# Decoder step on one Trainium2 core: value stores moved to the end of the attention stage, two value pages put behind four key pages, key quarters and three vector instructions put in another order

## The chip, the cores and the metric

The kernel runs on one core of one Trainium2 chip. The metric is the device time of one execution in microseconds (us), as the median over the runs of one version; lower is better. Five engines work side by side in a core: TensorE (PE; the loading of its weights is listed as PEld), VectorE (DVE), ScalarE (ACT), GpSimd (POOL) and SyncE (SP). Each takes its own instructions in the order in which they are written and waits on semaphores for the others. Transfers between the main memory and the on-chip memories are issued by SP and by ACT, each on a queue of its own (q1 and q10 in the profile), and are carried out by 16 DMA engines that both queues share.

## What is computed

One inference step of a small decoder, for one prompt of 512 tokens with 16 learned tokens ahead of it, and for 8 running sequences of 8 new tokens each with 1024 cached tokens. Layer one is a retention layer, layer two an attention layer with forget gates; each is followed by an MLP with a squared ReLU. Cut to what matters here:

```
x = x + retention_out(retention(...)); x = x + mlp(x)          # layer 1
k, v, logf = fox_shared_kv(x)          # new keys and values, both also outputs
q, gate = fox_in(x)
# prompt: causal attention of 16 heads over k, v
# 8 sequences: attention over 1024 cached rows, cache_k[page_table] and
#   cache_v[page_table] (8 pages of 128 rows each), and over the new k, v
p = softmax(q k^T * scale + cum_q - cum_k, masked);  o = p v
x = x + (o * sigmoid(gate)) @ w_fox_out
x = x + mlp(x)                         # layer 2
mlp(x) = square(relu(rms_norm(x, g) @ w_up)) @ w_down
```

All 592 tokens (64 new ones of the sequences, 16 learned, 512 of the prompt) go through the weights together. The outputs are the new activations, the retention states, and the new keys, values and log forget values.

## The kernel before, in words

The program is written out by hand, engine by engine: `block.sync` (SP), `block.gpsimd`, `block.tensor`, `block.scalar` (ACT) and `block.vector` (DVE) each hold the list of what their engine does, and the waits between them. Nothing reorders it later. Products of 32-bit numbers are made of three TensorE products of a high and a low part of each operand (`unit`, `unit_tok`, `unit_by_sums`): ACT rounds the high part of a weight block (`w_hi`), POOL or DVE subtracts it for the low part (`split`, `weight_low`).

**The attention stage** comes after the last block of the weights for the values (block N_V + 3). It is a pipeline of 9 rounds, b from 0 to 8, of 4 slots each, i from 0 to 3. A slot takes one of 32 pieces of the prompt's attention (j, a pair of heads and a block of 128 queries, by `pair_at`) and two of the 8 key pages of sequence b, and beside that the value pages of sequence b - 1.

- A *key page* holds 128 cached rows of 1024 numbers. `k_page` (L668) fetches it in four quarters of 128 KB, each a transfer of its own: quarter `a` takes four of the heads, in pieces of 1 KB, to partitions 32a to 32a + 31. There are 4 buffers for key pages. DVE waits for all four quarters and turns the page (`turn_page`, L2321), which raises `k_turned`; SP waits for that in `k_next` (L679) before it issues the page that is four further on. PE takes two turned pages at a time in `pair_scores`.
- A *value page* of 512 KB is one transfer (`v_page`, L674). There are 8 buffers. SP issues the first eight; the later ones ACT issues in `v_next`, when PE has used a buffer.
- In SP's list the first four key pages come first, then (when the last block of weights is done) the eight first value pages, the seventh behind a wait for `qb_done` and the eighth behind one for `kn_done`, and then key page 4 and the others through `k_next`.
- ACT issues the outputs before its own loop: the new log forget values and keys (`out_f`, `out_k`), and, when the last values have left PSUM, the new values (`out_v`, L1743): 2048, 64 and 256 KB. It then makes the exponentials (`exp`, L1750) and scales the probabilities with the inverse row sums (`normed_probs`, L1758).
- DVE, in each slot (from L2360): the row maxima of piece j (`maximum`), a page, the reciprocals of the row sums (`inverse_sums`, L2308), another page, and the gating of the piece before. In round 0 the first two slots hold no piece; slot 2 holds piece 0 and pages 4 and 5.
- Behind its loop ACT rounds the first block of the output projection (`w_hi(Blk(N_OUT))`), and waits for all stores of `out_f` and `out_v`.

**The MLP** is done in four chunks. In the last three the first matrix is multiplied by a scheme with seven block products in place of eight (`unit_by_sums` on PE; on DVE the list in `chunk`, from L2143). A chunk has four such units, j from 0 to 3. DVE adds a product in three steps, of which PE waits for the second and third (`prod_read`), and between them it makes the weights of the next unit: their sums, the low parts (`weight_low`, L2064, where j < 3) and the low parts of the sums (`sums_low`, L2070). There are two MLPs, so the unit j = 0 comes six times.

## Time and profile before

| | |
|---|---|
| time, median of 3 runs | 2080.22 us (2076.53 to 2080.82) |
| the profiled execution's own time | 2071.38 us |
| its span, first to last instruction | 2069.6 us |
| mean granted TensorE clock | 0.977 |
| PE busy | 1949.4 us, 94% of the span |
| DVE, ACT, POOL busy | 1049.0, 706.6 and 475.8 us |
| read from and written to the main memory | 210.77 and 26.12 MB |
| time of the packets of SP's queue and of ACT's queue, as a share of 16 engines | 29.5% and 8.1% |

The profile is that of one execution. A row of a timeline gives the start and the duration in us, the engine, the line of the program, the operation and its tiles; in brackets stands how long the engine was idle just before and what ended the idle time. "SPq" and "ACTq" are the engines' own sequencers, where transfers are issued; an issue row says how long issuing took, not when the data landed. Spans of matmuls overlap, so start times say more than sums of durations.

### The profile page before, as it was taken

To read this page: it belongs to the slowest core of one execution; us is meant where nothing else is said; L and a number is where in the kernel's file an instruction comes from. 1 tells how busy PE (TensorE), PEld (TensorE's weight loads), DVE (VectorE), ACT (ScalarE), POOL (GpSimd) and SP (SyncE) were. 2 spreads that over 40 slices of the span, in tenths; PEclk is the share of its full clock that TensorE was granted. 3 is DMA by queue.
4 is the path that set the end of the run, shared out by engine and by line. 5 is a ranking of instruction groups with operands and counts; after the bars stand their busy time and mean duration, and the time that the engine had idled before them with its cause. 6 is when DMAs were issued, how large, how long until landed. Compare 5 with 4: busy or idle time off the path is not lost.

```text
span 2069.6 us, 35725 instructions
## 1 busy us (share of the span) xinstructions
PE 1949.4 (94%) x14855; PEld 1789.2 (86%) x14855; DVE 1049.0 (51%) x1170; ACT 706.6 (34%) x898; POOL 475.8 (23%) x106
## 2 busy tenths in 40 slices
PE   3999999999998999999999999789998999999998
PEld 3988988988878999999999999645555999999998
DVE  2456245245346666464542535465664566736452
ACT  3132222222224425152432432144444332425241
POOL 1221521511505321212132232000000332021211
PEclk9999999999999999999999999879999999999999
DMA  4233233243342222222322221679997322322231
GB/s 137 82 111 135 92 126 129 83 135 120 102 153 82 82 80 84 82 87 76 109 78 82 63 65 60 228 192 268 280 266 204 95 81 80 102 82 81 81 102 46
DMA packets 197349, 239.13 MB, mean 116 GB/s; under 512 B 16419, under 2 KB 168355, under 8 KB 197027
## 3 DMA queue, kind: packets, MB, share of 16 engines
q1 hardware_dynamic: 171138, 183.25, 29.5%
q10 hardware_dynamic: 26000, 53.48, 8.1%
q8 instruction: 98, 1.61, 0.3%
q0 software_dynamic: 80, 0.52, 0.1%
q14 instruction: 33, 0.26, 0.0%
HBM read 210.77 MB, written 26.12 MB: 114 GB/s over the span
## 4 chain that ended last, share of the span: by engine, by line
PE 58%; issue 26%; DVE 5%; POOL 4%; DMA 4%; SPq 2%; ACT 1%; ACTq 0%; POOLq 0%; DVEq 0%
PE PS L782 10%; PE PS L784 10%; PE PS L783 10%; POOL w_lo L728 4%; PE PS L798 4%; PE PS L800 4%; PE PS L799 4%; DMA k_page<-in_cache_k 3%; PE PS L861 3%; PE PS L863 2%; PE PS L862 2%; PE PS L1303 1%; PE PS L1258 1%; SPq L671 1%; PE PS L1204 1%
## 5 line engine op out<-in xcount | busy, mean ns | idle before, releaser
L728 POOL TENSOR_TENSOR w_lo<-w_raw,w_hi 128x2048 fp32r<-128x2048 f32 (+1 forms) x101 | 474.6, 4699 | 1561.2 <-ACT w_hi L1407 1561.2
L1407 ACT ACTIVATE w_hi<-w_raw 128x2048 fp32r<-128x2048 f32 (+1 forms) x101 | 191.8, 1899 | 630.1 <-PE PS L784 418.8
L782 PE MATMUL PS<-hidden_hi,w_hi 128*128 128x296 f32 (+1 forms) x1024 | 304.4, 297 | 0.7 <-DVE hidden_tmp L2092 0.6
L784 PE MATMUL PS<-hidden_hi,w_lo 128*128 128x296 f32 (+1 forms) x1024 | 304.7, 298 | 0.0
L783 PE MATMUL PS<-hidden_lo,w_hi 128*128 128x296 f32 (+1 forms) x1024 | 304.2, 297 | 0.0
L782 PE MATMUL PS<-x_hi,w_hi 128*128 128x296 f32 (+1 forms) x896 | 271.0, 302 | 9.2 <-DVE x_lo L1856 6.1
L783 PE MATMUL PS<-x_lo,w_hi 128*128 128x296 f32 (+1 forms) x896 | 269.4, 301 | 0.0
L784 PE MATMUL PS<-x_hi,w_lo 128*128 128x296 f32 (+1 forms) x896 | 268.6, 300 | 0.0
L861 PE MATMUL PS<-w_hi,x_hi 128*128 128x256 f32 x800 | 226.5, 283 | 0.4 <-DVE fox_gate L2242 0.4
L863 PE MATMUL PS<-w_lo,x_hi 128*128 128x256 f32 x800 | 225.6, 282 | 0.0
L862 PE MATMUL PS<-w_hi,x_lo 128*128 128x256 f32 x800 | 225.3, 282 | 0.0
L782 PEld LDWEIGHTS PS<-hidden_hi,w_hi 128*128 128x128 f32 x1024 | 193.1, 189 | 1.6 <-issue 1.0
L783 PEld LDWEIGHTS PS<-hidden_lo,w_hi 128*128 128x128 f32 x1024 | 193.2, 189 | 0.0
L784 PEld LDWEIGHTS PS<-hidden_hi,w_lo 128*128 128x128 f32 x1024 | 192.6, 188 | 0.0
L782 PEld LDWEIGHTS PS<-x_hi,w_hi 128*128 128x128 f32 x896 | 170.3, 190 | 11.8 <-DVE x_lo L1856 7.4
L783 PEld LDWEIGHTS PS<-x_lo,w_hi 128*128 128x128 f32 x896 | 170.2, 190 | 0.3
L784 PEld LDWEIGHTS PS<-x_hi,w_lo 128*128 128x128 f32 x896 | 170.1, 190 | 0.0
L861 PEld LDWEIGHTS PS<-w_hi,x_hi 128*128 128x128 f32 x800 | 151.3, 189 | 1.1 <-issue 1.0
L863 PEld LDWEIGHTS PS<-w_lo,x_hi 128*128 128x128 f32 x800 | 151.4, 189 | 0.0
L862 PEld LDWEIGHTS PS<-w_hi,x_lo 128*128 128x128 f32 x800 | 151.2, 189 | 0.0
L2092 DVE TENSOR_TENSOR hidden_tmp<-PS,inv_root 128x1184 f32<-128x1184 f32 (+1 forms) x32 | 44.0, 1374 | 178.3 <-PE PS L784 178.0
L1414 ACT ACTIVATE w_hi<-w_raw 128x2048 fp32r<-128x2048 f32 x24 | 46.0, 1918 | 202.9 <-DVE w_raw L2055 202.9
(288 smaller groups left out, 3893.9 us busy)
## 6 DMA issues: line engine op xcount, KB each, us to landing
w_raw<-in_w_mlp_up SPq DMA_DIRECT2D x32, 1024.0 KB, 5.4
w_raw<-in_w_mlp_down SPq DMA_DIRECT2D x32, 1024.0 KB, 5.1
k_page<-in_cache_k SPq DMA_DIRECT2D x256, 128.0 KB, 6.6
v_page<-in_cache_v ACTq DMA_DIRECT2D x56, 512.0 KB, 8.5
w_raw<-in_w_ret_in SPq DMA_DIRECT2D x24, 1024.0 KB, 5.3
sample_state<-in_state_ret SPq DMA_DIRECT2D x32, 512.0 KB, 4.9
out_state_ret_sample<-sample_state ACTq DMA_DIRECT2D x32, 512.0 KB, 4.4
w_raw<-in_w_ret_out SPq DMA_DIRECT2D x16, 512.0 KB, 3.4
```

What stands on the lines that cost most here:

```text
L728: pool.tensor_tensor(lo, raw, hi.bitcast(F32), ALU.subtract).then_inc(lo_done, 1)
L782: pe.matmul(o, wh[:, w], xh[:, t, cols], start=(t == 0), stop=False)
L783: pe.matmul(o, wh[:, w], xl[:, t, cols], start=False, stop=False)
L784: last = pe.matmul(o, wl[:, w], xh[:, t, cols], start=False, stop=(t == kt - 1))
L798: pe.matmul(o, wh[:, t], xh[:, t], start=first and t == 0, stop=False, skip_group_check=True)
L799: pe.matmul(o, wh[:, t], xl[:, t], start=False, stop=False, skip_group_check=True)
L800: last = pe.matmul(o, wl[:, t], xh[:, t], start=False, stop=(t == 3), skip_group_check=True)
L861: pe.matmul(o, XH[:, t, tok], wh[:, c], start=start, stop=False, skip_group_check=skip)
L862: pe.matmul(o, XL[:, t, tok], wh[:, c], start=False, stop=False, skip_group_check=skip)
L863: return pe.matmul(o, XH[:, t, tok], wl[:, c], start=False, stop=(t == KT - 1), skip_group_check=skip)
L1407: act.activation(part(WH[n.slot], n), part(WR[n.slot], n), ACT.Copy).then_inc(hi_done, 1)
L1414: act.activation(WH[n.slot][:], WR[n.slot][:], ACT.Copy).then_inc(hi_done, 1)
```

## The change

Five edits, none of which changes what is computed.

1. `out_v` is issued by ACT behind its attention loop, ahead of `w_hi(Blk(N_OUT))`, on a semaphore of its own (`v_stored`). DVE waits for it ahead of the second MLP, whose buffers lie where the values were.
2. SP issues six value pages, then key pages 4 to 7 (as their buffers come free), then value pages 6 and 7, then the rest.
3. The quarters of a key page are issued in the order 0, 2, 1, 3.
4. In round 0 DVE makes the reciprocals of a piece ahead of the first of the slot's two pages.
5. In the MLP's unit j = 0 DVE makes the low parts of the next weights behind the second addition of the product, not ahead of it.

```
+        v_stored = sem("v_stored")
...
-            def k_page(kn, quarters=range(4)):
+            def k_page(kn, quarters=(0, 2, 1, 3)):
...
-                    k_page(NPAGE * b + p + NKS, range(4))
+                    k_page(NPAGE * b + p + NKS)
...
-            for i in range(NVS):
-                if i == 6:
-                    sp.wait_ge(qb_done, 1)
-                if i == 7:
-                    sp.wait_ge(kn_done, 1)
+            for i in range(6):
                 v_page(i)
             for b in range(DB + 1):
                 for p in range(4):
                     k_next(b, p)
+                if b == 0:
+                    sp.wait_ge(qb_done, 1)
+                    v_page(6)
+                    sp.wait_ge(kn_done, 1)
+                    v_page(7)
...
-            for dst, src in out_v:
-                act.dma_start(dst, src).then_inc(out_stored, 16)
...
+            for dst, src in out_v:
+                act.dma_start(dst, src).then_inc(v_stored, 16)
             w_hi(Blk(N_OUT))
-            act.wait_ge(out_stored, 16 * 6)
+            act.wait_ge(out_stored, 16 * 3)
...
-            act.wait_ge(out_stored, 16 * 6)
+            act.wait_ge(v_stored, 16 * 3)
...
-                        if j < 3:
+                        if 0 < j < 3:
                             weight_low(m + 1)
                         dve.wait_ge(sum_done, 2 * u + 1)
                         dve.wait_ge(prod_ready, 6 * u + 3)
                         dve.tensor_tensor(tmp[:, 1, 1], c, tmp[:, 0, 1], ALU.add).then_inc(prod_read, 1)
+                        if j == 0:
+                            weight_low(m + 1)
...
+                    if live(j) and b == 0:
+                        inverse_sums(j)
                     if k:
                         turn_page(NPAGE * b + 2 * i)
-                    if live(j):
+                    if live(j) and b > 0:
                         inverse_sums(j)
...
             roots(3)
+            dve.wait_ge(v_stored, 16 * 3)
             mlp(N_MLP1, 1)
```

SP's list at the start of the attention stage, before (key pages 4 and 5 go into the buffers k_page_144 and k_page_145; v_page_148 to v_page_155 are the eight buffers of value pages):

```order
L676 DMA v_page_152<-in_cache_v 128x1024
...
L676 DMA v_page_153<-in_cache_v 128x1024
...
L676 DMA v_page_154<-in_cache_v 128x1024
...
L676 DMA v_page_155<-in_cache_v 128x1024
...
L671 DMA k_page_144<-in_cache_k 32x4x256
```

and in the changed kernel:

```order
L677 DMA v_page_153<-in_cache_v 128x1024
...
L672 DMA k_page_144<-in_cache_k 32x4x256
...
L672 DMA k_page_145<-in_cache_k 32x4x256
...
L672 DMA k_page_146<-in_cache_k 32x4x256
...
L672 DMA k_page_147<-in_cache_k 32x4x256
...
L677 DMA v_page_154<-in_cache_v 128x1024
...
L677 DMA v_page_155<-in_cache_v 128x1024
```

Four key pages, 16 quarters, now stand ahead of the last two value pages.

DVE's list in round 0, slots 2 and 3, before:

```order
L2304 TENSOR_REDUCE neg_max<-PS 128x1
L2321 STREAM_TRANSPOSE k_page_t<-k_page_144 128x1024
L2308 RECIPROCAL row_inv<-row_sum 128x2
L2321 STREAM_TRANSPOSE k_page_t<-k_page_145 128x1024
L2302 TENSOR_TENSOR PS<-PS,c_fox_sb 128x128
```

and in the changed kernel:

```order
L2308 TENSOR_REDUCE neg_max<-PS 128x1
L2312 RECIPROCAL row_inv<-row_sum 128x2
L2325 STREAM_TRANSPOSE k_page_t<-k_page_144 128x1024
L2325 STREAM_TRANSPOSE k_page_t<-k_page_145 128x1024
L2306 TENSOR_TENSOR PS<-PS,c_fox_sb 128x128
```

The reciprocal no longer stands behind a page that has yet to arrive.

DVE's list in the MLP's unit j = 0 (hidden_tmp is the product, w_lo the next unit's weights), before:

```order
L2156 TENSOR_TENSOR hidden_tmp_89<-PS,hidden_tmp_89 128x296
L2064 TENSOR_TENSOR w_lo_55<-w_raw_51,w_hi_54 128x2048
...
L2161 TENSOR_TENSOR hidden_tmp_89<-PS,hidden_tmp_89 128x296
...
L2164 TENSOR_TENSOR hidden_tmp_89<-PS,hidden_tmp_89 128x296
...
L2070 TENSOR_TENSOR w_sum_lo_108<-w_sum_109,w_sum_hi_107 128x1536
```

and in the changed kernel:

```order
L2158 TENSOR_TENSOR hidden_tmp_89<-PS,hidden_tmp_89 128x296
...
L2163 TENSOR_TENSOR hidden_tmp_89<-PS,hidden_tmp_89 128x296
L2066 TENSOR_TENSOR w_lo_55<-w_raw_51,w_hi_54 128x2048
...
L2168 TENSOR_TENSOR hidden_tmp_89<-PS,hidden_tmp_89 128x296
...
L2072 TENSOR_TENSOR w_sum_lo_108<-w_sum_109,w_sum_hi_107 128x1536
```

The long subtraction stands between the second and the third addition now, not between the first and the second.

## Rows read from the trace of the kernel before

**Rows 1.** The waits of PE, whole span: engine, tile, line, releaser: us, times, longest.

```profile
PE PS L1221 <- ACT probs L1758: 16.0, 7, 14.9
...
PE PS L798 <- DVE hidden_tmp L2161: 7.6, 6, 1.3
```

**Rows 2.** Timeline of DVE at the start of the attention stage.

```profile
1349.33 1.25 DVE L2321 STREAM_TRANSPOSE k_page_t<-k_page 128x1024 f32<-128x1024 f32 x1 [17.02 <-DMA k_page<-in_cache_k]
...
1351.59 1.25 DVE L2321 STREAM_TRANSPOSE k_page_t<-k_page 128x1024 f32<-128x1024 f32 x1 [0.97 <-DMA k_page<-in_cache_k]
```

**Rows 3.** Timeline of ACT at the same place, ACTq its issues.

```profile
1327.54 1.17 ACTq L1744 DMA_DIRECT2D out_v_prompt<-fox_v  x2
1328.74 1.52 ACTq L1744 DMA_DIRECT2D out_v_sample<-fox_v  x1
...
1333.78 0.20 ACT L1750 ACTIVATION_READ_ACCUMULATOR probs<-PS,neg_max 128x1 f32 x1
1350.66 0.72 ACT L1758 ACTIVATE probs<-probs,row_inv 128x144 f32<-128x144 f32 x2 [16.68 <-DVE row_inv L2308]
```

**Rows 4.** Timeline of SP's issues at the same place.

```profile
1325.02 11.85 SPq L676 DMA_DIRECT2D v_page<-in_cache_v  x8
1338.48 14.52 SPq L671 DMA_DIRECT2D k_page<-in_cache_k  x19
```

**Rows 5.** The transfers from 1326 to 1344: all packets.

```profile
DMA packets 2188, 6.72 MB, mean 373 GB/s; under 512 B 469, under 2 KB 595, under 8 KB 2188
```

**Rows 6.** Timeline of PE behind the wait: pages 4 and 5, next piece's scores.

```profile
1352.89 1.93 PE L1258 MATMUL PS<-k_page_t,q_blocks 128*32 128x256 f32 x16 [0.77 <-DVE k_page_t L2321]
...
1356.10 1.01 PE L1200 MATMUL PS<-cum_parts,negsel_r 128*128 128x384 f32 x2
```

**Rows 7.** Timeline of DVE: maxima of a sequence's scores, rounds 2, 3, 4 and 8.

```profile
1395.15 1.29 DVE L2328 TENSOR_REDUCE neg_max<-PS 128x1 f32<-128x1088 f32 x1
1424.92 1.29 DVE L2328 TENSOR_REDUCE neg_max<-PS 128x1 f32<-128x1088 f32 x1
1459.13 1.29 DVE L2328 TENSOR_REDUCE neg_max<-PS 128x1 f32<-128x1088 f32 x1
...
1580.51 1.29 DVE L2328 TENSOR_REDUCE neg_max<-PS 128x1 f32<-128x1088 f32 x1
```

**Rows 8.** Transfers from 1346 to 1350, key quarters alone: all packets.

```profile
DMA packets 992, 0.90 MB, mean 226 GB/s; under 512 B 110, under 2 KB 992, under 8 KB 992
```

**Rows 9.** Transfers from 1603 to 1608, weight blocks alone: all packets.

```profile
DMA packets 1790, 1.82 MB, mean 363 GB/s; under 512 B 16, under 2 KB 1790, under 8 KB 1790
```

**Rows 10.** Timeline of DVE in one MLP unit j = 0.

```profile
781.54 0.47 DVE L2156 TENSOR_TENSOR hidden_tmp<-PS,hidden_tmp 128x296 f32<-128x296 f32 x1 [0.94 <-ACT hidden_tmp L1608]
781.92 2.28 DVE L2064 TENSOR_TENSOR w_lo<-w_raw,w_hi 128x2048 fp32r<-128x2048 f32 x1
784.12 0.46 DVE L2161 TENSOR_TENSOR hidden_tmp<-PS,hidden_tmp 128x296 f32<-128x296 f32 x1
784.70 0.47 DVE L2164 TENSOR_TENSOR hidden_tmp<-PS,hidden_tmp 128x296 f32<-128x296 f32 x1
```

**Rows 11.** Timeline of PE in the same unit.

```profile
783.06 0.30 PE L800 MATMUL PS<-x_hi,w_lo 128*128 128x296 f32 x1
784.63 0.41 PE L798 MATMUL PS<-x_hi,w_hi 128*128 128x296 f32 x1 [1.27 <-DVE hidden_tmp L2161]
...
786.37 0.30 PE L798 MATMUL PS<-x_hi,w_sum_hi 128*128 128x296 f32 x1
```

**Rows 12.** Timelines of ACT, POOL and PE at the end of the attention stage.

```profile
1594.39 1.89 ACT L1407 ACTIVATE w_hi<-w_raw 128x2048 fp32r<-128x2048 f32 x1
...
1596.36 4.54 POOL L728 TENSOR_TENSOR w_lo<-w_raw,w_hi 128x2048 fp32r<-128x2048 f32 x1 [298.65 <-ACT w_hi L1407]
...
1605.57 0.58 PE L782 MATMUL PS<-fox_y_hi,w_hi 128*128 128x288 f32 x1 [2.24 <-DVE fox_y_lo L2389]
```

**Rows 13.** Windows, 1352 to 1373: engines' busy us, granted clock, DMA share, GB/s.

```profile
1352.00:1373.00 21.00, 20.18 (x119) 11.50 (x119) 12.37 (x24) 7.98 (x22) 0.00 (x0) 0.59 0.67 168
```

## The prediction

> **What bounds the kernel now.** I read four views, in this order. First the waits of PE, since PE is busy for 94% of the span and time can only be had where it is not: one wait of 14.9 us stands out, on ACT's scaled probabilities (L1758), and one kind comes six times, 7.6 us in all, on DVE's second addition in the MLP (L2161) [rows 1]. Second the timelines of the engines around the long wait, to follow it back. DVE had the row maxima of the first piece done at 1332.3 and then stood for 17.02 us in front of the transpose of key page 4, until its data were there at 1349.33 [rows 2]. The reciprocal that ACT needed stood behind that transpose: ACT had the exponentials done at 1333.98 and waited 16.68 us [rows 3]. SP shows why the page was late: its first quarter was issued at 1338.48 only, behind eight value pages whose issues took from 1325.02 on, while ACT issued the stores of the values from 1327.54 on [rows 4, 3]. All told 6.72 MB went through the DMA engines from 1326 to 1344, at 373 GB/s [rows 5].
>
> Third the pace of the rounds behind it. The maxima of a sequence's scores come once a round. The round from 1395.15 to 1424.92 took 29.77 us; the six rounds from 1395.15 to 1580.51 took 185.36 us, which is 6.7 us more than six of the short one [rows 7]. So this stretch is bound by the engines' own chain for most of the time, and by late key pages for 6.7 us at most. Fourth the timelines of one MLP unit j = 0, for the waits that come six times [rows 10, 11].
>
> **Stores and value pages at the start.** Behind the change six value pages stand ahead of key page 4, not eight, and the stores (2048 + 64 + 256 KB = 2.42 MB) are gone from there. Two value pages are 1.05 MB. 3.47 MB at the 373 GB/s of [rows 5] are 9.3 us, by which key page 4 comes earlier. The other key pages keep their distance to it, since quarters alone drain at 226 GB/s [rows 8], 2.3 us a page, about the 2.26 us between the transposes of pages 4 and 5 [rows 2]. What PE does next hangs on page 5: its product of pages 4 and 5 began at 1352.89, the next piece's scores at 1356.10 [rows 6]; all of that moves with page 5. I take **9.3 us**. The bounds: 2.8 us, if the stores ran in time that SP's issues left free and only the two value pages count; 14.9 us, the whole wait of PE.
>
> Value pages 6 and 7 land later now, but PE wants them in round 1, some 30 us on: nothing. Key page 8 is new behind them, 2.8 us of transfers. Before, it was asked for when page 4 was turned (1349.33 + 1.25 [rows 2]) and is turned in round 1, behind maxima of scores that PE only began at 1356.10 [rows 6]; 5.5 us and the length of the scores lie between, of which the page itself takes 2.3; what is left covers the 2.8 about. Nothing, with 1.5 us as the upper end.
>
> **Reciprocals first.** In round 0 ACT and PE now get piece 0 done while the pages are on their way. But the product of pages 4 and 5 stands next in PE's list [rows 6], so the path still waits for page 5: I give it nothing beyond the 9.3 us. It has a price: page 6 is turned behind the second reciprocal, so behind the second pair of exponentials; I put that at 1.25 us, the length of the transpose with which it changes place [rows 2]. The product of pages 6 and 7 comes only behind the scores that began 3.2 us after page 4 and 5's [rows 6], which hides it.
>
> **Order of the quarters.** Nothing in the trace shows another order, so this is bounded. Key quarters and weight blocks come in pieces of the same 1 KB; the quarters, on 32 partitions each, drain at 226 GB/s [rows 8], weight blocks on 128 at 363 GB/s [rows 9]. Whatever costs the quarters that factor of 1.6 may be eased when one quarter's neighbours in the queue lie elsewhere. The upper end in the rounds is the 6.7 us above, because then the chain of the engines binds; the lower end is nothing, or a loss (the third rival). Even a tenth off a page is 8 x 0.23 = 1.8 us a round, more than most rounds have over 29.77, so I take a value nearer to the upper end: **4 us**.
>
> The Trainium skill, page "SBUF — State Buffer", section "Door 1: The DMA port swizzle", says that partitions 0 to 63 reach no more ports than 0 to 31, and that 64 to 127 reach the other half. By that rule the old order sends two quarters in a row to one half of the ports, the new order alternates, and the whole upper end could come (second rival). The same page, section "Can I just issue two DMAs to hit both halves?", speaks against it: two transfers at once, one on each half, were only 6% faster than one. By that 6% a page would save 0.14 us, an estimate, and the sum below would be nearer to 2062. The rows show the gap between the two shapes, and nothing of the order.
>
> **The MLP unit.** PE needs the second addition when its product ends, at 783.06 + 0.14 = 783.20, and the third 1.74 us later (784.63 to 786.37 is such a product) [rows 11]. Before, the second addition stood behind 2.28 us of low parts and ended at 784.58; PE began at 784.63, and the next product at 786.37. Now the second addition can start 0.58 us after the first started (the distance of second and third, 784.12 to 784.70 [rows 10]), at 782.12, and ends at 782.58, ahead of PE. The low parts follow from 782.50 to 784.78, the third addition ends at about 785.17, and PE goes on at 785.22, having waited some 0.3 us. That is 1.15 us less than 786.37. DVE's list from there is as early as before, so nothing behind it is later. Six units [rows 1], **6.9 us**, in a stage where PE has nothing else to wait for. The bounds: nothing, and the 7.6 us of the row.
>
> **The stores at the end.** ACT now issues three stores ahead of rounding the first output block. Issuing took 1.17 + 1.52 us [rows 3]. POOL finished its part at 1600.90 and PE began that block at 1605.57, behind another wait [rows 12]: 4.67 us of room. The transfers, 6.5 us at the rate above, go beside the weights of blocks that PE reaches some 15 us later. DVE's new wait comes some 50 us later. Nothing, unless issuing takes over 4.7 us; then the excess is lost, 3 us at most by a like queue.
>
> **The sum.** 9.3 + 4 + 6.9 = 20.2 us. The profiled execution took 2071.38 us and would take 2051.2; it lay 8.8 us under the median of 2080.22, and I take the difference over to that: **2060.0 us**. What a measurement of this kernel can tell from no change is about 0.2%, 4.2 us.
>
> **Rivals.**
> 1. *The stores were not what delayed the page.* SP's value pages went out one by one over 11.85 us [rows 4]; if that pace is SP's own, only two issues fall away. For it: the issues are evenly spread. Against it: the DMA engines moved 373 GB/s all that time [rows 5], so that they were hardly waiting for SP. Then 2.8 + 4 + 6.9 = 13.7, 2066.5 us. 13%.
> 2. *The quarters run at the rate of weight blocks.* A page takes 1.44 us in place of 2.32: the 6.7 us go whole, and pages 4 and 5 come 1.8 us earlier still. 9.3 + 1.8 + 6.7 + 6.9 = 24.7, 2055.5 us. For it: the factor of 1.6 [rows 8, 9]. 
> 3. *Slower: the new order makes key quarters slower.* The place is the rounds 1 to 8, 56 key pages, where little room is left. If a page takes longer by d, some 56 x d are lost, and from d = 0.29 us (an eighth of 2.32) on the 16.2 us of the other edits are gone; at a quarter, 0.58 us, 32 are lost and 2096 us come out. For it: the four quarters of a page are neighbouring KB of the same rows, and the new order reads them in jumps. Against it: all four are issued within 3 us or so either way, and both orders read the same pieces. 4%.
> 4. *The MLP edit only moves the wait*, to the third addition, for instance because the subtraction runs longer beside the second's readers. Then 13.3, 2066.9 us. For it: by my sum 0.3 us of waiting stays there anyway. Against it: all durations are measured and none changes. 8%.
>
> The clock is open too: from 1352 to 1373 the granted clock was 0.59 [rows 13], mostly the lower of its levels of 1.2 and 2.4 GHz, behind the long idle of PE. A shorter idle may keep less of it low, at most some 5 us for the better; I count nothing, but let the range reach there.
>
> **How the numbers follow.** The forecast has 60%, the rivals 13, 12, 4 and 8, and 3 are left for no visible effect. The range of 2050 to 2070 holds the forecast with its ends (order of the quarters nothing: 2064; with a late key page or a late end: 2067), rivals 1, 2 and 4, and on the low side the second with part of the clock; some 1 in 7 is left out. Faster by over 0.2%: 0.92; within: 0.04; slower: 0.04.
>
> **What would show it.** Right: DVE's wait ahead of page 4 of about 7 to 8 us, not 17; ACT's scaling of the first piece within a us of its exponentials; no wait of PE on the second addition, and one of 0.3 us on the third; in the stretch of the rounds a mean round between 29.8 and 30.9 us; PE's first output block still released by DVE. Wrong: page 4 transposed later than 1344 on the old clock; a stretch of only key quarters below 226 GB/s; PE's first output block released by POOL.

## The result and the profile after

Four runs of the changed kernel gave a median of 2049.55 us (2047.84 to 2056.13), four of the kernel before 2080.52 us (2076.53 to 2087.0): a ratio of 0.9854, 95% interval 0.9821 to 0.9887. The forecast was 2060.0 us, 2050 to 2070: the direction is right, the gain larger, the time 0.45 us below the range. In a later set with more runs (11 and 28) the ratio was 0.9895 [0.9864, 0.9926], a gain of 21.8 us where 20.2 were forecast. The kernel before spreads by itself, from 2060 to 2094 us over 91 later runs, and the time goes with the mean granted TensorE clock of the run: 0.980 in the shortest, 0.965 in the longest, a correlation of -0.89 over the 91.

The profiled executions took 2071.38 and 2048.63 us, spans 2069.6 and 2046.8. The difference by places: DVE's first page turns, the start of the attention stage, came 6.2 us earlier (1326.65, now 1320.42); from there to the first maxima of a sequence's scores passed 28.08 us, not 37.77; the seven rounds between the first and the last such maxima took 214.84 us, not 216.09; and what follows 483.46, not 489.09. 6.2 + 9.7 + 1.3 + 5.6 = 22.8 us. Ahead of the attention stage and behind it only the MLP edit acts, and 6.2 + 5.6 = 11.8 us is more than its 6.9; what is over belongs to these two executions (the last sections).

DVE's timeline at the start of the attention stage, changed kernel:

```profile
1320.42 4.58 DVE L2325 STREAM_TRANSPOSE k_page_t<-k_page 128x1024 f32<-128x1024 f32 x4
...
1327.78 0.17 DVE L2312 RECIPROCAL row_inv<-row_sum 128x2 f32<-128x2 f32 x1 [1.70 <-ACT probs L1750]
1333.65 1.25 DVE L2325 STREAM_TRANSPOSE k_page_t<-k_page 128x1024 f32<-128x1024 f32 x1 [5.70 <-DMA k_page<-in_cache_k]
1335.67 1.25 DVE L2325 STREAM_TRANSPOSE k_page_t<-k_page 128x1024 f32<-128x1024 f32 x1 [0.78 <-DMA k_page<-in_cache_k]
```

These answer to [rows 2]: the wait ahead of page 4 is 5.70 us, not 17.02 (7.4 with the wait that now comes first, for the exponentials that the reciprocal needs). Page 5 is turned 15.25 us after the first pages; before it was 24.94. On ACT's timeline the scaling of the first piece stands 0.23 us behind the exponentials, where [rows 3] show 16.68:

```profile
1327.98 0.72 ACT L1758 ACTIVATE probs<-probs,row_inv 128x144 f32<-128x144 f32 x2 [0.23 <-DVE row_inv L2312]
```

What PE waits for now, whole span (columns as in [rows 1]):

```profile
PE PS L1260 <- DVE k_page_t L2325: 6.5, 1, 6.5
...
PE PS L1223 <- ACT probs L1758: 1.2, 6, 0.2
PE PS L800 <- DVE hidden_tmp L2168: 1.1, 4, 0.3
```

The 14.9 us on the probabilities are gone, and 6.5 us on pages 4 and 5 have come in their place. The waits on the second addition are gone, and the third has four, none over 0.3 us, as forecast. SP's issues at the same place, against [rows 4]:

```profile
1318.79 5.88 SPq L677 DMA_DIRECT2D v_page<-in_cache_v  x6
1325.45 9.68 SPq L672 DMA_DIRECT2D k_page<-in_cache_k  x16
1335.90 1.48 SPq L677 DMA_DIRECT2D v_page<-in_cache_v  x2
```

The rounds, by the maxima as in [rows 7], on DVE's timeline (first, third to seventh, and last):

```profile
1348.50 1.29 DVE L2332 TENSOR_REDUCE neg_max<-PS 128x1 f32<-128x1088 f32 x1
...
1411.73 1.29 DVE L2332 TENSOR_REDUCE neg_max<-PS 128x1 f32<-128x1088 f32 x1
1441.49 1.29 DVE L2332 TENSOR_REDUCE neg_max<-PS 128x1 f32<-128x1088 f32 x1
1471.24 1.29 DVE L2332 TENSOR_REDUCE neg_max<-PS 128x1 f32<-128x1088 f32 x1
1501.00 1.29 DVE L2332 TENSOR_REDUCE neg_max<-PS 128x1 f32<-128x1088 f32 x1
1530.76 1.29 DVE L2332 TENSOR_REDUCE neg_max<-PS 128x1 f32<-128x1088 f32 x1
1563.34 1.29 DVE L2332 TENSOR_REDUCE neg_max<-PS 128x1 f32<-128x1088 f32 x1
```

Four rounds in a row take 29.75 or 29.76 us, the length of the shortest round of before; the mean of seven is 30.7 (29.8 to 30.9 forecast).

The unit j = 0 of the MLP, DVE's timeline and then PE's, against [rows 10, 11]:

```profile
778.70 0.47 DVE L2158 TENSOR_TENSOR hidden_tmp<-PS,hidden_tmp 128x296 f32<-128x296 f32 x1 [0.94 <-ACT hidden_tmp L1610]
779.29 0.47 DVE L2163 TENSOR_TENSOR hidden_tmp<-PS,hidden_tmp 128x296 f32<-128x296 f32 x1
779.67 2.28 DVE L2066 TENSOR_TENSOR w_lo<-w_raw,w_hi 128x2048 fp32r<-128x2048 f32 x1
781.87 0.46 DVE L2168 TENSOR_TENSOR hidden_tmp<-PS,hidden_tmp 128x296 f32<-128x296 f32 x1
```

```profile
782.38 0.41 PE L800 MATMUL PS<-x_hi,w_sum_hi 128*128 128x296 f32 x1 [0.24 <-DVE hidden_tmp L2168]
```

The second addition starts 0.59 us after the first (0.58 forecast); PE waits 0.24 us for the third. And the end of the stage, ACT's issues and then PE, against [rows 12]:

```profile
1576.76 0.41 ACTq L1810 DMA_DIRECT2D out_v_prompt<-fox_v  x1
...
1577.20 0.52 ACTq L1810 DMA_DIRECT2D out_v_prompt<-fox_v  x1
1577.76 1.05 ACTq L1810 DMA_DIRECT2D out_v_sample<-fox_v  x1
```

```profile
1588.07 0.58 PE L784 MATMUL PS<-fox_y_hi,w_hi 128*128 128x288 f32 x1 [2.24 <-DVE fox_y_lo L2395]
```

The first output block is still released by DVE, behind the same 2.24 us. The stores cost nothing there.

### The profile page after: what moved, and what is told of

Its sections match the earlier page's. It is cut to its first block, busy times and chain, and to the rows that moved or that the text cites. A ratio compares the mean times of both kernels' runs of the same rounds, so it can differ in the third digit from the quotient of the medians.

```text
span 2046.8 us, 35726 instructions
## 1 busy us (share of the span) xinstructions
PE 1942.6 (95%) x14855; PEld 1782.9 (87%) x14855; DVE 1050.3 (51%) x1170; ACT 705.8 (34%) x898; POOL 476.1 (23%) x106
## 4 chain that ended last, share of the span: by engine, by line
PE 60%; issue 26%; DVE 6%; POOL 4%; ACT 1%; DMA 1%; ACTq 1%; SPq 0%; POOLq 0%; DVEq 0%
PE PS L784 10%; PE PS L785 10%; PE PS L786 10%; POOL w_lo L730 4%; PE PS L800 4%; PE PS L802 4%; PE PS L801 4%; PE PS L863 3%; PE PS L864 3%; PE PS L865 3%; PE PS L1305 1%; PE PS L1260 1%; PE PS L1206 1%; DVE k_page_t L2325 1%; PE PS L1240 1%
## 5 line engine op out<-in xcount | busy, mean ns | idle before, releaser
L784 PEld LDWEIGHTS PS<-x_hi,w_hi 128*128 128x128 f32 x896 | 169.5, 189 | 11.9 <-DVE x_lo L1858 7.6
```

The source lines that it names most:

```text
L784: pe.matmul(o, wh[:, w], xh[:, t, cols], start=(t == 0), stop=False)
```

## The experiments

Three sets of four kernels, each timed beside the kernel before on one chip: its medians were 2072.90 us (29 runs), 2076.48 (28) and 2075.73 (34). The table gathers what DVE's timelines show: the transposes of page 5 and the first maxima, from the first page turns; the seven rounds from first to last maxima; DVE's waits for key pages within those; the mean granted clock over those; and the rate in 4 us that hold only key quarters. The rounds and the waits are those of one trace each. Names with a_ start from the changed kernel, with b_ from the kernel before.

| kernel | page 5, us | maxima, us | seven rounds, us | waits there, us | clock there | GB/s | median us (runs) | ratio to before |
|---|---|---|---|---|---|---|---|---|
| before | 24.9 | 37.8 | 216.1 | 15.6 | 0.97 | 226 | 2080.52 (4) | |
| the change | 15.3 | 28.1 | 214.8 | 1.8 | 0.96 | 261 | 2049.55 (4) | 0.9854 [0.9821, 0.9887] |
| before_again | 23.7 | 36.2 | 218.5 | 6.6 | 0.95 | 240 | 2074.87 (12) | 1.0005 [0.9983, 1.0026] |
| a_order_0123 | 16.0 | 28.9 | 225.1 | 11.9 | 0.93 | 231 (241 in a window 1 us later) | 2058.55 (6) | 0.9935 [0.9916, 0.9954] |
| b_stores_pages | 15.7 | 28.5 | 223.7 | 9.7 | 0.93 | 236 | 2065.62 (12) | 0.9975 [0.9951, 0.9999] |
| b_mlp | 24.0 | 36.5 | 219.6 | 7.0 | 0.95 | 231 | 2067.79 (12) | 0.9976 [0.9953, 0.9999] |
| after_again | 14.9 | 27.4 | 215.0 | 2.8 | 0.97 | 260 | 2053.61 (11) | 0.9895 [0.9864, 0.9926] |
| a_order_0312 | 15.1 | 28.0 | 211.7 | 3.3 | 0.97 | 251 | 2051.98 (6) | 0.9883 [0.9842, 0.9924] |
| a_order_1032 | 15.0 | 27.8 | 227.0 | 15.9 | 0.92 | 233 | 2062.93 (12) | 0.9939 [0.9906, 0.9971] |
| b_order | 22.7 | 34.8 | 209.0 | 3.4 | 1.00 | 265 | 2066.35 (12) | 0.9968 [0.9937, 0.9999] |
| a_no_recip | 15.0 | 27.5 | 217.4 | 0.3 | 0.95 | 265 | 2051.99 (12) | 0.9897 [0.9866, 0.9928] |
| a_v_behind | 8.7 | 32.4 | 222.2 | 2.3 | 0.92 | | 2060.62 (12) | 0.9924 [0.9895, 0.9954] |
| a_v_behind_low | 8.7 | 32.3 | 216.6 | 5.0 | 0.95 | | 2057.94 (11) | 0.9917 [0.9889, 0.9946] |
| b_stores | 17.6 | 30.1 | 213.9 | 11.1 | 0.98 | 234 | 2068.82 (12) | 0.9972 [0.9943, 1.0001] |

**before_again**, the kernel before with nothing changed.

> The kernel before, once more, to see how its executions differ: the changed kernel's profiled execution was 22.8 us shorter than that of before, but its median 31 us. Theory: before's executions differ in how long the wait ahead of key page 4 and the waits for later key pages are, and the profiled one was a good one; then this profile shows a span over 2069.6 us with the excess in the attention stage (DVE waiting for key pages more than the 34.3 us in all of the first profile). Rival: the stretches outside the attention stage differ (retention, MLP); then the key page waits stay at 34 us within 2. Ratio 1.000 within 0.003 either way.

The ratio is 1.0005. One trace of a kernel is one draw: the waits for key pages in the rounds were 6.6 us here, 15.6 in the first trace. The expectation on where executions differ is not borne out: this span is 10.3 us shorter than the first, 7.1 us of it ahead of the attention stage and 4.0 behind, while the rounds are 2.4 us longer in spite of the shorter waits.

**a_order_0123**, the changed kernel with the old order of the quarters:

```
-            def k_page(kn, quarters=(0, 2, 1, 3)):
+            def k_page(kn, quarters=(0, 1, 2, 3)):
```

> The changed kernel with the quarters back in the order 0, 1, 2, 3. Theory: the order makes key quarters drain faster (255 to 263 GB/s in the changed kernel's stretch of quarters alone, 226 before), so this run drains at 226 again, page 5 is turned about 1.5 us later behind the start of the stage, and DVE waits some 10 to 15 us for key pages in rounds 1 to 8 (under 1 us in the changed kernel); 4 to 7 us slower than the changed kernel, ratio to before 0.987 to 0.989. Rival: the order does nothing, the pages came sooner because the stores were gone; then the drain stays over 250 GB/s and the time stays that of the changed kernel, ratio 0.985.

Its ratio is 0.9935, that of the changed kernel 0.9895 in the second set and 0.9854 in the first: the order is worth 8 us or more behind the other four edits, over the 4 to 7 expected, though this compares sets from different chips (a_order_1032 below does it within one set). Page 5 comes 0.8 us later; what is lost is lost in the rounds. DVE's waits from 1356 to 1582, then the same row of the changed kernel from 1348 to 1565:

```profile
DVE k_page_t L2325 <- DMA k_page<-in_cache_k: 11.9, 10, 1.9
```

```profile
DVE k_page_t L2325 <- DMA k_page<-in_cache_k: 1.8, 3, 1.0
```

No wait is over 1.9 us, yet one round took 38.49 us (maxima at 1505.52 and 1544.01), 8.7 over the short one. PE's wait in that round, then its windows (columns as in [rows 13]):

```profile
1509.96 0.40 PE L1227 MATMUL PS<-c_keep_sb,probs 128*32 128x128 f32 x1 [2.84 <-DVE fox_gate L2318]
```

```profile
1505.00:1513.00 8.00, 4.97 (x23) 2.17 (x22) 3.19 (x6) 3.54 (x7) 0.00 (x0) 0.71 1.04 341
1513.00:1521.00 8.00, 7.94 (x27) 4.52 (x26) 3.41 (x7) 2.83 (x6) 0.00 (x0) 0.50 1.09 274
1521.00:1529.00 8.00, 8.00 (x74) 5.33 (x77) 4.12 (x7) 2.73 (x9) 0.00 (x0) 0.73 0.59 152
```

A page came 1.68 us late, the gating behind it on DVE too, and PE stood for 2.84 us (to 1509.96). The granted clock fell within the first of these windows, was at 0.50, the lower of its two levels, in the second, and came back within the third. So this round lost more than the wait.

**b_stores_pages**, the kernel before with edits 1 and 2 alone:

```
-            for dst, src in out_v:
-                act.dma_start(dst, src).then_inc(out_stored, 16)
...
+            for dst, src in out_v:
+                act.dma_start(dst, src).then_inc(v_stored, 16)
             w_hi(Blk(N_OUT))
...
-            for i in range(NVS):
+            for i in range(6):
...
+                if b == 0:
+                    sp.wait_ge(qb_done, 1)
+                    v_page(6)
+                    sp.wait_ge(kn_done, 1)
+                    v_page(7)
```

> The kernel before with the first two edits alone (stores at the end, two value pages behind four key pages). Theory: the 9.7 us by which page 5 came earlier in the changed kernel are due to these two; the distance from the first transpose to that of page 5 goes from 24.9 us to about 16.5, the waits for later key pages stay, the MLP waits stay at 7.6 us; 8 to 10 us faster, ratio 0.995 to 0.996. Rival: the reciprocals ahead of the turns are needed for it; then under 5 us, ratio over 0.9975.

Page 5 comes at 15.7 us, the first maxima 8 to 9 us earlier than before, but the time falls by 5 us only (0.9975, interval 0.2 to 10 us): the rounds that follow took 223.7 us. Three kernels have an early start and quarters in the old halves; their rounds are 225.1, 223.7 and 227.0 us, the longest of the table, at granted clocks of 0.92 and 0.93. The rival, that the reciprocals are needed for it, falls with a_no_recip below, where the whole gain comes without them.

**b_mlp**, the kernel before with edit 5 alone:

```
-                        if j < 3:
+                        if 0 < j < 3:
                             weight_low(m + 1)
...
+                        if j == 0:
+                            weight_low(m + 1)
                         dve.wait_ge(prod_read, 2 * u + 1)
```

> The kernel before with the last edit alone (low parts of the weights behind the second addition in unit j = 0). Theory: six times 1.15 us are gone: 6.9 us faster, ratio 0.9967; PE's waits on the second addition go from 7.6 us to none, on the third some 0.3 us each at most. Rival: the wait only moves to the third addition; then PE's waits for it sum to over 5 us and the ratio is over 0.999.

PE's waits in the unit fall from 7.6 to 1.1 us (4 times, 0.3 at most), and the time by 5.0 us (0.2 to 9.7). 6.9 lies inside; the runs can't size it better, the row of waits can: 6.5.

**after_again**, the changed kernel once more.

> The changed kernel once more, to learn how far its own rounds repeat. If the rounds at the engines' floor belong to the new order, the seven rounds between the maxima of the sequences again sum to 215 us or so (7 x 29.76 = 208.3, and a dip of the clock or two at some 3 us each), and DVE's waits for key pages behind round 1 stay below 3 us. If the first trace was a lucky one, the sum is 218 to 225 us with over 6 us of such waits, as in the three traces with the old order. The ratio to the kernel before should be 0.9854 to within 0.4%.

Rounds of 215.0 us and waits of 2.8 us: the new order's rounds repeat.

**a_order_0312** and **a_order_1032**, the changed kernel with two more orders:

```
-            def k_page(kn, quarters=(0, 2, 1, 3)):
+            def k_page(kn, quarters=(0, 3, 1, 2)):
```

```
-            def k_page(kn, quarters=(0, 2, 1, 3)):
+            def k_page(kn, quarters=(1, 0, 3, 2)):
```

> The changed kernel with its key quarters in the order 0, 3, 1, 2. Theory A, it is the alternation between partitions 0 to 63 and 64 to 127 that counts: the order alternates as 0, 2, 1, 3 does, so the time is that of the changed kernel within 3 us, the rounds sum to 215 us, and DVE's waits for key pages behind round 1 stay below 3 us. Theory B, it is the source that counts, quarters that are not neighbours in a row: 3 and 1, 0 and 3, 1 and 2 are neighbours in one place only, so between the two, 2 to 5 us slower than the changed kernel. Theory C, chance: nothing tells the four orders apart, and all lie within 3 us of each other.

> The changed kernel with its key quarters in the order 1, 0, 3, 2: two of the low partitions, then two of the high ones, and no quarter behind its lower neighbour. Theory A, the alternation counts: this is as slow as 0, 1, 2, 3, so 8 to 9 us slower than the changed kernel, rounds of 222 to 226 us in sum, and over 8 us of DVE's waits for key pages behind round 1. Theory B, only ascending neighbours hurt (a source read straight on): as fast as the changed kernel, within 3 us. Theory C, chance: within 3 us of the order 0, 3, 1, 2.

Theory A holds, with small misses in size (waits of 3.3 us where under 3 were expected, rounds of 211.7 for 215 and of 227.0 for 222 to 226). 0, 3, 1, 2 alternates between the lower and the upper 64 partitions and is as fast as the change; 1, 0, 3, 2 takes two of a half in a row, never reads straight on, and is as slow as 0, 1, 2, 3: 9 us slower than the change by the medians of the same set. The table splits without overlap: all seven kernels with alternating quarters wait 0.3 to 5.0 us for key pages in the rounds, the other seven 6.6 to 15.9; quarters alone run at 251 to 265 GB/s or at 226 to 241.

A rival that these times leave open: neighbours in the source, either way round, are slow behind each other. 0, 1, 2, 3 has three such pairs a page and 1, 0, 3, 2 two, the two fast orders have one, so it sorts the four orders as theory A does. The rate inside a page tells them apart. In 0, 1, 2, 3 the half changes twice a page (1 to 2, and 3 to 0 of the next page), but only the second of these steps joins quarters that are no neighbours; so theory A expects two fast spells a page, the rival one. GB/s in slices of 0.1 us, b_stores_pages (order 0, 1, 2, 3) from 1338, then the changed kernel from 1331.5:

```profile
GB/s 236 225 215 205 205 246 195 277 317 256 287 205 225 225 205 215 225 215 297 307 287 266 225 215 215 205 215 184 225 307 297 297 246 246 184 215 236 195 215 256
```

```profile
GB/s 205 256 307 297 246 205 256 287 318 236 215 246 297 297 236 236 225 318 318 225 225 236 307 297 215 246 246 307 318 215 225 225 318 297 246 215 205 348 307 236
```

In the first the fast spells come every 1.1 us, half of a page's 2.2, and in the second every 0.5 us, a quarter of 2.0: at each change of half. That speaks for theory A. The pattern is weaker in the other traces with two quarters of a half in a row, and hardly to be seen in before.

The transfers of the two kernels where only key quarters run, all packets; first a_order_0312 from 1337 to 1341:

```profile
DMA packets 1104, 1.01 MB, mean 251 GB/s; under 512 B 123, under 2 KB 1104, under 8 KB 1104
```

and a_order_1032 from 1337 to 1341:

```profile
DMA packets 1022, 0.93 MB, mean 233 GB/s; under 512 B 114, under 2 KB 1022, under 8 KB 1022
```

In the rounds, beside value pages, the quarters land after 6.1 us (a_order_0312, median from issue, 1362 to 1570) and 7.2 (a_order_1032):

```profile
k_page<-in_cache_k SPq DMA_DIRECT2D x200, 128.0 KB, 6.1
```

```profile
k_page<-in_cache_k SPq DMA_DIRECT2D x200, 128.0 KB, 7.2
```

**b_order**, the kernel before with edit 3 alone:

```
-            def k_page(kn, quarters=range(4)):
+            def k_page(kn, quarters=(0, 2, 1, 3)):
...
-                    k_page(NPAGE * b + p + NKS, range(4))
+                    k_page(NPAGE * b + p + NKS)
```

> The kernel before with the order of the quarters alone changed to 0, 2, 1, 3. The long wait ahead of page 4 stays, 21 to 23 us from the first transposes to those of page 4. Theory A, the order is worth something by itself in the rounds: DVE's waits for key pages behind round 1 fall from 7 to 16 us to below 3 us, the rounds sum to 211 to 215 us, and the time is 4 to 9 us below the kernel before, a ratio of 0.996 to 0.998. Rival, the order counts only once the start is cleared (the rounds before were late by at most 6.7 us, and a start that is late anyway leaves the queue time to catch up): ratio 0.999 to 1.001. On the upper end in the prediction the gain is 6.7 us at most.

Theory A: rounds of 209.0 us, 29.9 on average, while the long wait at the start stays. The time falls by 6.6 us (0.2 to 13.1). So the order pays without the cleared start as well. The size is less sure from the trace, the only one of the fourteen whose rounds held the full clock (1.00).

**a_no_recip**, the changed kernel without edit 4:

```
-                    if live(j) and b == 0:
-                        inverse_sums(j)
                     if k:
                         turn_page(NPAGE * b + 2 * i)
-                    if live(j) and b > 0:
+                    if live(j):
                         inverse_sums(j)
```

> The changed kernel without the fourth edit: in round 0 the reciprocals stand behind the page turns again, and the rest is as changed. Forecast: ACT's scaling of the first piece waits for page 4 again, by some 5 to 7 us, but PE's product of pages 4 and 5 still waits for page 5, so the first maxima of round 1 come 28 us after the first transposes as in the changed kernel (27.4 to 28.1), and the time is the same within 3 us. Rival: the probabilities' products, now behind page 5's turn, add to that chain, and it is 3 to 6 us slower, with the first maxima at 31 us or later.

As forecast: ACT waits again, PE waits 5.6 us for it, and only 0.5 for pages 4 and 5, which had cost 6.5. ACT's timeline, then PE's two rows of waits:

```profile
1339.10 0.72 ACT L1758 ACTIVATE probs<-probs,row_inv 128x144 f32<-128x144 f32 x2 [7.01 <-DVE row_inv L2312]
```

```profile
PE PS L1223 <- ACT probs L1758: 6.8, 7, 5.6
...
PE PS L1260 <- DVE k_page_t L2325: 0.5, 1, 0.5
```

The first maxima come as early, and the ratio is that of the change. The edit moves a wait and takes none away.

This trace also shows that the length of the rounds is not the sum of the waits for pages. b_order has the same order of quarters and 3.4 us of such waits, this kernel 0.3, and its rounds are 8.4 us longer. The rounds of b_order and then of a_no_recip, first to last maxima (columns as in [rows 13]):

```profile
1363.81:1572.82 209.01, 196.16 (x2017) 116.20 (x2016) 142.49 (x287) 98.73 (x281) 0.00 (x0) 1.00 0.98 265
```

```profile
1352.29:1569.68 217.39, 205.48 (x2017) 120.50 (x2016) 142.14 (x287) 98.70 (x280) 0.00 (x0) 0.95 0.94 258
```

The difference is the granted clock, 1.00 and 0.95. Without rounding, 208.3 us and the time lost to the clock (one less the granted clock, times the stretch; an estimate) give the rounds of all fourteen traces to about 3 us.

**a_v_behind**, the changed kernel with all value pages behind key pages 4 to 7:

```
-            for i in range(6):
-                v_page(i)
             for b in range(DB + 1):
                 for p in range(4):
                     k_next(b, p)
                 if b == 0:
+                    for i in range(6):
+                        v_page(i)
                     sp.wait_ge(qb_done, 1)
```

> The changed kernel with all eight first value pages behind key pages 4 to 7, not two. Six value pages are 3.15 MB. If bytes ahead in the queue are what delays page 4 (the theory), it comes some 7 us earlier, 6 us after the first transposes in place of 13, PE loses its wait of 6.5 us ahead of the product of pages 4 and 5, and the time is 5 to 6 us below the changed kernel's. Rival: the value pages become the next late thing, PE waits for them in round 1, and nothing or less than 2 us is left.

A miss: a ratio of 0.9924 beside 0.9895 and 0.9897, so 6 us slower than the changed kernel (8.6 by the medians, against a_no_recip of the same set), and in neither of the two ways named. Page 5 came at 8.7 us, and PE's 6.5 us went, as the theory has it. But key page 8 stood behind eight value pages now. SP's issues, then DVE and PE, a round later:

```profile
1337.28 8.11 SPq L677 DMA_DIRECT2D v_page<-in_cache_v  x8
1346.17 3.83 SPq L672 DMA_DIRECT2D k_page<-in_cache_k  x6
```

```profile
1355.76 1.25 DVE L2325 STREAM_TRANSPOSE k_page_t<-k_page 128x1024 f32<-128x1024 f32 x1 [14.12 <-DMA k_page<-in_cache_k]
1356.93 0.12 DVE L2312 RECIPROCAL row_inv<-row_sum 128x2 f32<-128x2 f32 x1
```

```profile
1357.77 1.54 PE L1223 MATMUL PS<-c_keep_sb,probs 128*128 128x128 f32 x6 [14.69 <-ACT probs L1758]
```

It is the long wait of the kernel before, with the reciprocal behind the page as there, one round on. Of these two splits, six value pages ahead and two behind was the better.

**a_v_behind_low**, that kernel with the low parts of unit j = 0 behind the third addition:

```
-                        if j == 0:
-                            weight_low(m + 1)
                         dve.wait_ge(prod_read, 2 * u + 1)
                         dve.wait_ge(prod_ready, 6 * u + 4)
                         dve.tensor_tensor(tmp[:, 1, 1], d, tmp[:, 1, 1], ALU.add).then_inc(prod_read, 1)
+                        if j == 0:
+                            weight_low(m + 1)
```

> The previous kernel, and the low parts in the MLP unit j = 0 behind the third addition, not the second. PE's waits on the third addition (1.1 us, 4 times, in the changed kernel) go away if the two low parts are what holds it up; the gain is 1 us in all, which this comparison can hardly tell. Rival: the low parts, later now, hold up the weights of the next block, and PE waits for those by up to 2.3 us a unit, 7 us slower than the previous kernel at the most.

No wait of PE on either addition is left, and none on the next weights came. The ratio to before is 0.9917 beside 0.9924; a gain of 1 us can't be told at this spread.

**b_stores**, the kernel before with edit 1 alone:

```
-            for dst, src in out_v:
-                act.dma_start(dst, src).then_inc(out_stored, 16)
...
+            for dst, src in out_v:
+                act.dma_start(dst, src).then_inc(v_stored, 16)
             w_hi(Blk(N_OUT))
```

> The kernel before with only the stores of the values moved to the end of the stage; all eight value pages stay ahead of key page 4. The stores are 2.42 MB, at 373 GB/s 6.5 us. If bytes delay the page, the transposes of page 4 come 15 to 16 us after the first ones in place of 21.5 to 22.7, and the time falls by 3 to 6 us. The first rival of the prediction (SP's own pace of issuing the value pages delays it, not the stores): page 4 stays at 21 us or later and the time does not change; then the two value pages behind the key pages were what gave the gain.

Page 4 comes 15.3 us after the first pages, so the stores were what delayed it. Page 5 comes 6.1 to 7.4 us earlier than in before_again and before (6.5 by bytes); the two value pages add 1.9 (17.6 against 15.7; 2.8 by bytes). DVE's timeline of b_stores, its first turns at 1334.16:

```profile
1349.47 1.25 DVE L2322 STREAM_TRANSPOSE k_page_t<-k_page 128x1024 f32<-128x1024 f32 x1 [9.65 <-DMA k_page<-in_cache_k]
1351.71 1.25 DVE L2322 STREAM_TRANSPOSE k_page_t<-k_page 128x1024 f32<-128x1024 f32 x1 [0.94 <-DMA k_page<-in_cache_k]
```

The time fell by 5.8 us in the middle, and the interval just reaches 1. Its rounds, 213.9 us, are the shortest of those with the old order, at a clock of 0.98 and with 11.1 us of waits, so that neither an early start nor such waits alone make them long; how far they go together stays open.

None of the kernels beats the change; a_order_0312 and a_no_recip equal it. Value pages between key pages 8 to 11, or the reciprocals ahead of the turns in round 1 as well, were not tried.

## Why the prediction was right, and where it was not

- **Stores and value pages, 9.3 us: right as far as page 5.** 9.7 us in the two profiles. As time, b_stores_pages gained 5 us (0.2 to 10), and its trace shows long rounds behind the early start. The prediction took the rounds as independent of the start. That is not shown: with the new order they took 211.7 to 217.4 us behind the early start and 209.0 behind the late one (b_order, one trace).
- **Reciprocals, nothing: right,** and for the reason given (a_no_recip).
- **Order of the quarters, 4 us: mis-sized, and by another path.** The failing sentence is "The upper end in the rounds is the 6.7 us above, because then the chain of the engines binds". The 6.7 us were six rounds of one trace over the shortest one, and not late pages alone: 4.4 of them are the round from 1424.92 to 1459.13 [rows 7], in which PE waited for 2.37 us and the clock was then low for 6.8 us. Over seven rounds (7 x 29.76 = 208.3 us) the three traces of kernels with the old start and old order (before, before_again, b_mlp) lie 7.8, 10.1 and 11.3 us over, those with edits 1 and 2 and two quarters of a half in a row 15.4 to 18.7, and b_stores, with edit 1 alone, 5.6. The mean of the seven non-alternating kernels is 220.5 us, that of the five alternating ones without the long stall of a_v_behind 213.6: **7 us** (leaving those two out is a choice; with them it is 5 us); by the runs 6.6 us alone (0.2 to 13.1) and 8 to 9 behind the other edits.

  Most of it goes with the clock, which the prediction had weighed only behind the start, and counted as nothing. PE waited over 2 us behind a late page, 2.37 to 3.09, in five rounds, all in kernels with two quarters of a half in a row. In four of them the clock fell around the wait, for 13.7 to 20.5 us, and in before 5 us behind it, for 6.8; these rounds took 34.2 to 40.9 us, and what they took over 29.76, 40.5 us in seven traces, is 5.8 us a trace, most of the 7. That the waits bring the falls is argued from this, not shown. Other falls of the clock are as many in either group, in eight rounds and in nine. The runs agree: the change (after_again) and a_order_1032, of one set, differ by 9.7 us in their mean span, and their mean granted clocks of 0.9785 and 0.9752 make 7 of it, an estimate as above.

  The step under it, a tenth off a page, was right: the means of the table's rates are 260 and 234 GB/s, 11%.
- **The MLP unit, 6.9 us: right.** 7.6 us of waits became 1.1; alone it gave 5.0 us, in an interval that holds 6.9.
- **The stores at the end, nothing: right** by the end rows of the profile.
- **The sum.** 20.2 us against 22.8 in the two profiles and 21.8 in the larger set of runs. The first agreement is partly luck: the rounds of the two profiles differ by 1.3 us where 4 were forecast, and the stretches ahead of and behind the attention stage by 11.8 where 6.9 were, with a granted clock of 0.98 behind it before and 0.99 after. Edits 1 and 2 together, 3 alone and 5 alone gained 5, 6.6 and 5 us, 17 of the 21.8, with intervals wide enough for either. The median after lies 10.5 us under the forecast mostly for another reason: 8.8 us were added because the profiled execution of before lay that far under its median. The profiled execution after took 2048.63 us, near its own median, so that the added part was not there; 2051.2 would have been the better forecast. The median of before was that of three runs, and high: the later medians are 2072.90 to 2076.48 us.
- **The rivals.** SP's pace (1) fell with b_stores. Weight-block rate (2) fell: 265 GB/s at most, not 363; but the rounds gained nearly what it had put there. Slower quarters (3) fell with b_order and a_order_0123, a moved MLP wait (4) with b_mlp.

What such a tenth is worth is the point: a page of 0.52 MB takes 2.02 us in place of 2.24, so a round of eight pages 1.8 us less. That was enough for no wait of PE over 2 us to come in the rounds, the stall of a_v_behind and a_v_behind_low apart, and the long falls of the clock beside such waits went with them.

The Trainium skill, page "SBUF — State Buffer", section "Door 1: The DMA port swizzle", says that partitions 0 to 63 share one half of the ports and 64 to 127 the other. The four orders agree with it: the two that alternate are fast, the two that don't are slow; no run shows a port. The Trainium skill, same page, section "Can I just issue two DMAs to hit both halves?", gives 6% more for two transfers at once, one on each half, than for one. No run here makes that comparison; the 11% between the orders is nearer to it than to the factor of 1.6 of the second rival, and the measurement decides.

## What to carry to other kernels

Ask of every transfer at a stage's start what stands behind it in the queue: 2.4 MB of stores that nobody waited for held up a page, an in-order engine behind it, and through that PE. Moving bytes behind one page puts them ahead of the next (a_v_behind), so split them where both have room. Where a stage repeats with little slack, look at how the order of small transfers lies over the partitions, and take the slack from several traces, with the granted clock beside each round: a long round is not a late page until its clock has been looked at.

## What was not expected of the hardware

Quarters of 32 partitions run faster when neighbours in the queue go to different halves of the partitions, 260 against 234 GB/s on average, and the plain order 0, 1, 2, 3 is one of the slow ones.

A wait of PE of 2.84 us came with a fall of the granted clock, to 0.50 and 0.73 in the windows of the next 16 us, and that round was 8.7 us longer than the short one. Four other rounds had waits of PE of 2.37 to 3.09 us, and a fall at them or soon after. The clock also falls without a late page: the changed kernel's round from 1378.82 to 1411.73 took 32.91 us, with no wait for a key page in it, and one window at little over half the clock:

```profile
1379.00:1386.70 7.70, 6.40 (x40) 3.73 (x37) 4.64 (x9) 3.36 (x8) 0.00 (x0) 0.99 1.07 312
```

```profile
1386.70:1394.00 7.30, 7.30 (x39) 3.84 (x38) 3.07 (x4) 3.34 (x8) 0.00 (x0) 0.54 0.85 253
1394.00:1402.00 8.00, 8.00 (x98) 5.18 (x102) 4.44 (x10) 2.98 (x11) 0.00 (x0) 1.00 0.64 186
```

PE had been busy for 6.40 of 7.70 us before it fell. What brings it down there is open.

Time moves between executions ahead of the attention stage too: its first page turns came from 1316.2 to 1334.2 us over the fourteen traces, in kernels that differ there by edit 5 alone. A part of it is again the clock (granted 0.98 ahead of the stage in b_stores, the latest, and 0.99 in a_v_behind_low, the earliest). No experiment went after that.
